# Mixing stage of a hybrid encoder step: the inverse's last level on one quadrant, decay sums of all tiles at once, and three changes of order on GpSimd and VectorE

## What is computed

```
def gdn_chunk(S, q, k, v, g, beta):
    gc = jnp.cumsum(g, axis=-1)
    decay = jnp.exp(jnp.where(lower, gc[..., :, None] - gc[..., None, :], -jnp.inf))
    kb = k * beta[..., None]
    lmat = jnp.where(strict, jnp.einsum('bhid,bhjd->bhij', kb, k) * decay, 0.0)
    t_inv = lax.linalg.triangular_solve(eye + lmat, eye, left_side=True, lower=True, unit_diagonal=True)
    u = t_inv @ (v * beta[..., None])
    w = t_inv @ (kb * jnp.exp(gc)[..., None])
    v_new = u - w @ S
    o = (q * jnp.exp(gc)[..., None]) @ S + (jnp.einsum('bhid,bhjd->bhij', q, k) * decay) @ v_new
    S_new = S * jnp.exp(g_last) + jnp.einsum('bhld,bhle->bhde', k * jnp.exp(g_last - gc), v_new)
```

## Time and profile before

| | us |
|---|---|
| median of 3 runs | 3766.71 (3763.04 to 3767.36) |
| profiled execution, its own time | 3768.46 |
| its span | 3766.8 |
| mixing, iterations without Y ahead of tile 0 | 1427 to 1566 |
| mixing, 23 iterations with all strands | 1604.2 to 2379.3 |
| mixing, 7 iterations without E, F (H in the first only) | 2379.3 to 2589.3 |

### The profile page before, as it was taken

The page is one execution under the profiler, slowest core; times in us unless marked ns, Lnnn a source line. Parts: engine busy times, 40 slices in busy tenths (PEclk is TensorE's granted clock), DMA queues, the critical chain, the costliest instruction groups (busy, mean ns, idle before and its releaser), DMA issues. The chain is left out here.

```text
span 3766.8 us, 66113 instructions
## 1 busy us (share of the span) xinstructions
PE 3191.2 (85%) x18658; PEld 1938.3 (51%) x18659; DVE 2155.4 (57%) x5335; ACT 1538.5 (41%) x3032; POOL 823.0 (22%) x1002
## 2 busy tenths in 40 slices
PE   8997979788797976699999999998499999999920
PEld 3443434333343456577777777766355555555500
DVE  6574757566665764477677777766433333333358
ACT  6464656556555662233333333332122222222222
POOL 0000000000000001255445554553111111111145
PEclk9998989899898985799999999999799999999965
DMA  4456656574747534445554455433367778985378
GB/s 144 142 182 224 213 194 231 184 258 164 274 159 243 190 127 144 121 138 148 145 146 129 130 145 149 131 112 92 132 223 252 269 266 283 324 295 185 110 275 333
DMA packets 487498, 716.00 MB, mean 190 GB/s; under 512 B 92272, under 2 KB 241360, under 8 KB 486992
## 3 DMA queue, kind: packets, MB, share of 16 engines
q1 hardware_dynamic: 404096, 480.63, 41.3%
q10 hardware_dynamic: 54288, 146.56, 9.8%
q0 software_dynamic: 28864, 86.09, 6.3%
HBM read 442.22 MB, written 270.92 MB: 189 GB/s over the span
## 5 line engine op out<-in xcount | busy, mean ns | idle before, releaser
L338 PE MATMUL pP<-h_hi,w_hi 128*128 128x512 f16 (+1 forms) x1728 | 639.0, 374 | 86.1 <-ACT win L430 67.1
L338 PE MATMUL pP<-h_lo,w_hi 128*128 128x512 f16 (+1 forms) x1728 | 637.6, 373 | 0.0
L338 PE MATMUL pP<-h_hi,w_lo 128*128 128x512 f16 (+1 forms) x1728 | 635.9, 372 | 0.0
L1863 PE MATMUL ebank<-w_halves,rowsT_hi 128*128 x1568 | 485.4, 381 | 1.5 <-ACT rowsT_hi L1899 0.9
L529 DVE SCALAR_TENSOR_TENSOR halves<-stage,halves 128x512 f16<-128x512 f32 x384 | 254.6, 687 | 200.6 <-ACT halves L400 200.4
L400 ACT ACTIVATE halves<-stage 128x512 f16<-128x512 f32 x384 | 236.4, 625 | 273.7 <-DMA stage<-in_raw 264.4
L569 DVE SCALAR_TENSOR_TENSOR cv<-win,cols_sb,cv 128x512 f32<-128x512 f32 (+1 forms) x432 | 305.5, 707 | 35.8 <-issue 1.4
L338 PEld LDWEIGHTS pP<-h_hi,w_hi 128*128 128x128 f16 x1728 | 174.6, 101 | 293.1 <-ACT win L430 80.4
L1863 PE MATMUL ebank<-w_halves,rowsT_lo 128*128 x784 | 298.9, 381 | 0.0
L298 POOL TENSOR_TENSOR ss<-ss,eps 128x4 f32<-128x4 f32 (+1 forms) x9 | 2.2, 249 | 1295.7 <-ACT junk L386 1295.7
L338 PEld LDWEIGHTS pP<-h_hi,w_lo 128*128 128x128 f16 x1728 | 175.1, 101 | 191.7 <-issue 18.3
(11 more groups left out here) (344 smaller groups left out, 6666.9 us busy)
## 6 DMA issues: line engine op xcount, KB each, us to landing
stage<-in_raw SPq DMA_DIRECT2D x384, 256.0 KB, 4.0
split<-halves SPq DMA_DIRECT2D x384, 256.0 KB, 3.3
w_halves<-split SPq DMA_DIRECT2D x32, 2048.0 KB, 11.6
y<-yb ACTq DMA_DIRECT2D x98, 512.0 KB, 7.4
ft<-mixin SPq DMA_DIRECT2D x33, 1280.0 KB, 8.5
mixin<-qo ACTq DMA_DIRECT2D x128, 256.0 KB, 3.7
w_halves<-split SPq DMA_DIRECT2D x32, 1024.0 KB, 6.1
xt<-in_x SPq DMA_DIRECT2D x33, 512.0 KB, 5.2
```

What stands on the lines that cost most here:

```text
L338: ins = nc.tensor.matmul(pP[n % NPB][:, 0:N], w[:, k, c0:c0 + P], h[:, k, 0:N], start=(k + i == 0), stop=(k == KD - 1 and i == 2))
L1863: ins = nc.tensor.matmul((M0, M1)[p][:, :], x[p][:, k, :], w[:, bass.ds(s, 1), k, half, :].rearrange("p a n -> p (a n)"), start=(k + i == ...
```

## The change

Three things are done. The decay sums of the 32 prompt tiles are made at the start of mixing, by three matmuls into one bank and three exponentials into `st_all`; `stat`, `gt`, `ex` and `fsc` lose that part for these tiles (the stream tile keeps it). At level 64 the mask, W64, I64, Z64 and its copy work on the one quadrant of 64 by 64 per head that is not known beforehand; Z32's copy now goes to `Zf`, which Z64 reads and completes. And three places of `MIX` change: `eT` comes after `r2`, `B32` before `h2` (both POOL), `on` before `fsc` (DVE).

```diff
-Q.sct0.pool X.eT.pool E.sq.act R.x2.dve Y.KS.pe Y.QS.pe Y.X.dve R.st.act Y.o1.act R.r2.pool X.B16.pool X.eZ.pool
+Q.sct0.pool E.sq.act R.x2.dve Y.KS.pe Y.QS.pe Y.X.dve R.st.act Y.o1.act R.r2.pool X.eT.pool X.B16.pool X.eZ.pool
-E.stat.pe E.sse.dve E.ex.act E.rr.pool Q.sct1.pool R.h2.pool
+E.stat.pe E.sse.dve E.ex.act E.rr.pool Q.sct1.pool X.B32.pool R.h2.pool
-R.lg.pe R.r0.dve X.T16.pe X.T16c.act X.B32.pool R.r1.dve
+R.lg.pe R.r0.dve X.T16.pe X.T16c.act R.r1.dve
-X.W32.pe X.I32.dve F.G.dve E.fsc.dve Y.outA1.pe Y.on.dve
+X.W32.pe X.I32.dve F.G.dve Y.on.dve E.fsc.dve Y.outA1.pe
...
                     for c in range(2 * H):
-                        nc.tensor.matmul(bank[:, c:c + SW], sqb[:, c, :], mat("ones")[:, 0:SW], start=True, stop=True)
-                    pe.wait_ge(*at("gt", t))
-                    c = 2 * H
-                    for m in ("upto_s" if stream else "upto", "after_s" if stream else "after", "ones"):
-                        ins = nc.tensor.matmul(bank[:, c:c + SW], mat(m), gw[:, :], start=True, stop=True)
-                        c += H
+                        ins = nc.tensor.matmul(bank[:, c:c + SW], sqb[:, c, :], mat("ones")[:, 0:SW], start=True, stop=True)
                     if stream:
+                        pe.wait_ge(*at("gt", t))
...
+                        if s == 64:
+                            ins = nc.tensor.matmul(XA[64:P, h, 0:64], Bs[s][0:64, h, 64:P], Tm[0:64, h, 0:64],
+                                                   start=True, stop=True)
...
-                        ins = nc.tensor.matmul(XB[:, h, :], WI[:, h, :], Zm[:, h, :], start=True, stop=True)
+                        ins = nc.tensor.matmul(XB[0:64, h, 64:P], WI[64:P, h, 0:64], Zf[p][64:P, h, 64:P],
+                                               start=True, stop=True)
...
             pe.wait_ge(const_in, 16)
+            for i, m in enumerate(("upto", "after", "ones")):
+                ins = nc.tensor.matmul(flat(XA)[:, i * last * H:(i + 1) * last * H], mat(m), gb[:, 0:last, H:], start=True, stop=True)
+            ins.then_inc(decays_made, 1)
...
                 elif n == "Z64c":
+                    act.wait_ge(*at("Z64", t))
+                    nc.scalar.activation(Zf[p][0:64, :, 64:P], XB[0:64, :, 64:P], ACT.Copy).then_inc(*did(n))
...
+            act.wait_ge(decays_made, 1)
+            for i in range(3):
+                ins = nc.scalar.activation(st_all[:, 0:last, (7 + i) * H:(8 + i) * H],
+                                           flat(XA)[:, i * last * H:(i + 1) * last * H].rearrange("p (t h) -> p t h", h=H), ACT.Exp)
+            ins.then_inc(decays_kept, 1)
...
-                    nc.gpsimd.tensor_tensor(Bs[s][:, :, :], Gin[:, :, :], heads(mat(f"level{s}")), ALU.mult
+                    rows, c0 = (64, 64) if s == 64 else (P, 0)
+                    mask = mat(f"level{s}")[0:rows, c0:P].unsqueeze(1).to_broadcast([rows, H, P - c0])
+                    nc.gpsimd.tensor_tensor(Bs[s][0:rows, :, c0:P], Gin[0:rows, :, c0:P], mask, ALU.mult
...
-                    nc.vector.tensor_copy(gt[p][:, :], gb[:, bass.ds(t, 1), :].rearrange("p a b -> p (a b)"))
-                    dve.drain()
-                    ins = nc.vector.tensor_copy(gw[:, 0:H], gt[p][:, H:])
+                    ins = nc.vector.tensor_copy(gt[p][:, :], gb[:, bass.ds(t, 1), :].rearrange("p a b -> p (a b)"))
...
+                    if n == "I64":
+                        nc.vector.tensor_copy(WI[64:P, :, 0:64], XA[64:P, :, 0:64]).then_inc(*did(n))
```

More of the change, by code:

```diff
@@ L1026, in f_step @@
                     for c in range(2 * H):
-                        nc.tensor.matmul(bank[:, c:c + SW], sqb[:, c, :], mat("ones")[:, 0:SW], start=True, stop=True)
-                    pe.wait_ge(*at("gt", t))
-                    c = 2 * H
-                    for m in ("upto_s" if stream else "upto", "after_s" if stream else "after", "ones"):
-                        ins = nc.tensor.matmul(bank[:, c:c + SW], mat(m), gw[:, :], start=True, stop=True)
-                        c += H
-                    if stream:
+                        ins = nc.tensor.matmul(bank[:, c:c + SW], sqb[:, c, :], mat("ones")[:, 0:SW], start=True, stop=True)
+                    if stream:
+                        pe.wait_ge(*at("gt", t))
+                        c = 2 * H
+                        for m in ("upto_s", "after_s", "ones"):
+                            nc.tensor.matmul(bank[:, c:c + SW], mat(m), gw[:, :], start=True, stop=True)
+                            c += H
                         ins = nc.tensor.matmul(bank[:, c:c + SB * H], mat("ones"),
@@ L1072, in x_step @@
                 elif n == "vt":
+                    pe.wait_ge(decays_kept, 1)
                     pe.wait_ge(*at("I64", t, 1))
@@ L1229, in f_step @@
                     act.wait_ge(*at("sse", t))
-                    ins = nc.scalar.activation(scf[p][:, 7:10, :].rearrange("p a h -> p (a h)"), flat(YE if prologue(t) else FB)[:, 2 * H:5 * H], ACT.Exp)
                     if stream:
-                        ins = nc.scalar.activation(exS[:, :], flat(FB)[:, 5 * H:5 * H + SB * H], ACT.Exp)
-                    ins.then_inc(*did(n))
+                        nc.scalar.activation(scf[p][:, 7:10, :].rearrange("p a h -> p (a h)"), flat(FB)[:, 2 * H:5 * H], ACT.Exp)
+                        nc.scalar.activation(exS[:, :], flat(FB)[:, 5 * H:5 * H + SB * H], ACT.Exp).then_inc(*did(n))
+                    else:
+                        act.sem_inc(*did(n))
                 elif n == "DT":
@@ L1254, in x_step @@
                 elif n == "Z64c":
+                    act.wait_ge(*at("Z64", t))
+                    nc.scalar.activation(Zf[p][0:64, :, 64:P], XB[0:64, :, 64:P], ACT.Copy).then_inc(*did(n))
+                elif n == "Z16c":
+                    act.wait_ge(*at("Z16", t))
+                    nc.scalar.activation(Zm[:, :, :], XA[:, :, :], ACT.Copy).then_inc(*did(n))
+                elif n == "Z32c":
                     act.wait_ge(*at("N", t, 2))
-                    act.wait_ge(*at("Z64", t))
+                    act.wait_ge(*at("Z32", t))
                     nc.scalar.activation(Zf[p][:, :, :], XB[:, :, :], ACT.Copy).then_inc(*did(n))
-                elif n in ("Z16c", "Z32c"):
-                    act.wait_ge(*at(n[:-1], t))
-                    nc.scalar.activation(Zm[:, :, :], (XA if n == "Z16c" else XB)[:, :, :], ACT.Copy).then_inc(*did(n))
                 elif n == "fh":
@@ L1404, in f_step @@
                     dve.wait_ge(*at("stat", t, 1))
-                    nc.vector.tensor_copy(gt[p][:, :], gb[:, bass.ds(t, 1), :].rearrange("p a b -> p (a b)"))
-                    dve.drain()
-                    ins = nc.vector.tensor_copy(gw[:, 0:H], gt[p][:, H:])
+                    ins = nc.vector.tensor_copy(gt[p][:, :], gb[:, bass.ds(t, 1), :].rearrange("p a b -> p (a b)"))
                     if stream:
+                        dve.drain()
+                        nc.vector.tensor_copy(gw[:, 0:H], gt[p][:, H:])
                         ins = nc.vector.tensor_tensor(
@@ L1490, in x_step @@
                     dve.wait_ge(*at(f"W{n[1:]}", t))
-                    nc.vector.tensor_tensor(WI[:, :, :], (XB if n == "I32" else XA)[:, :, :], heads(mat("ident")), ALU.add
-                                            ).then_inc(*did(n))
+                    if n == "I64":
+                        nc.vector.tensor_copy(WI[64:P, :, 0:64], XA[64:P, :, 0:64]).then_inc(*did(n))
+                    else:
+                        nc.vector.tensor_tensor(WI[:, :, :], (XB if n == "I32" else XA)[:, :, :], heads(mat("ident")), ALU.add
+                                                ).then_inc(*did(n))
                 if n == "I64" and stream:
```

18 lines of the change are left out of this document (12 added, 6 removed).

## The result

| | before | after |
|---|---|---|
| median, us (4 runs each) | 3767.03 | 3742.78 (3740.33 to 3743.71) |
| profiled execution, its own time / span | 3768.46 / 3766.8 | 3743.71 / 3742.1 |
| first stat to first KS (ahead of tile 0) | 132.7 | 122.7 |
| iteration of tile 0 | 38.06 | 40.33 |
| 23 iterations with all strands | 775.07 (33.70 each) | 752.45 (32.72 each) |

The ratio is 0.9936 (95% interval 0.9919 to 0.9953): 24 us faster, where 50 were forecast. The stretches are taken between the starts of KS in the two traces, as in the earlier trace rows. The 23 iterations gained 22.6 us instead of 44, 0.98 each instead of 1.9. Ahead of tile 0 it is 10.0 instead of 4; the last seven lost 2.3, where 2 were to be gained, and tile 0's iteration, which the sum leaves out, lost 2.3. (Mixing began 1.8 us later, what follows it took 1.6 longer.)

What follows compares the result with a forecast made beforehand. The prediction took the loop from kt over G to ft's landing, beside PE, as the bound. Gains of 44 (23 iterations), 4 (ahead of tile 0) and 2 (last seven) made 50 us: 3717 us, range 3690 to 3748.

Steps and rivals of the forecast that it cites:

- Ahead of tile 0: Term for the stretch before the first tile: decay sums made at once gain 4 us net, between -2 and +6.
- the last seven: Term for the seven iterations without E and F: 0.3 us gained in each, 2 us together, between -3 and +6.
- the loop: kt to G, then G to ft landed: 33.3 of 33.7 us, falling to 31.8; 1.9 per iteration, 44 us in 23.
- W32's wait: Sign: PE's W32 no longer waits on POOL (1.89 us); T32 waits 1 to 2 us for DVE's I32 instead.
- `on` alone: Step moving `on` before fsc on DVE: oT's wait of 0.73 us goes, but counts nothing by itself.
- xn is short: Sign on DVE: xn takes well below its former duration.
- r2 before eT: Step on POOL: r2 starts at 2009.6, takes 0.95 us; what stood behind both starts 0.4 earlier.
- B32 before h2: Step on POOL: `goh` ends with B32, `esel` meets h2; I32 1.67 us earlier, G 1.5 earlier after kt.
- the signs foretold: Expected in the profile after: `esel` median near 2 us, `goh` below 0.93, `dif` near 0.21, periods 31 to 32.5.
- The first rival: r1 on DVE runs free, `esel` not held by h2; G gains up to 3.5 us: 3680 us, 9%.
- the second rival: The power inside ro on POOL also holds DVE; r1 loses up to 1.0 us more: 3740 us, 12%.
- the fifth rival: Longer pauses of PE ahead of T32 drop its granted clock to the lower level: slower, 3790 us, 5%.

Runs made afterwards that it cites:

- e8_on_only: The kernel before with only `on` moved ahead of fsc on VectorE; ratio 1.0003 to the kernel before.
- e15_drain_h2: The changed kernel with a drain added on GpSimd between B32 and h2; ratio 0.9883 to the kernel before.
- e1_fence: The changed kernel with the drain between r2's two GpSimd instructions replaced by a semaphore; ratio 0.9888 to the kernel before.
- e2_h2late: The changed kernel with h2 behind ro on GpSimd, waiting for r1, and ACT's sh and rx behind T32's copy; ratio 0.9835 to the kernel before.
- The kernel with both POOL edits: The changed kernel with r2's drain replaced by a semaphore and h2 moved behind ro and r1; ratio 0.9789 to the kernel before.
- e14_store_behind: The kernel with both POOL edits, with only G's large store moved behind the load ft on SP; ratio 0.9790 to the kernel before.

## Why the prediction was right and wrong

**Right: the loop, once the change is in.** kt to G (18.9) and G to ft (13.6) make 32.4 of the 32.72 us, kt waits for ft in 12 iterations and KS for `off` in the 11 with V, and what moved G then moved the period: with kt to G of 18.9, 18.2, 18.1, 16.9 and 16.4 the iterations take 32.72, 32.04, 31.84, 31.11 and 30.65. Right too: W32's wait goes and T32 waits for I32 (2.0 us); `on` alone is worth nothing; xn is short (0.85).

In the kernel before the loop was looser than the one iteration that the prediction followed. The means of the 23 are 19.2 and 13.7, 32.9 of 33.70 us, and kt waited for ft once. So of the 0.98 us that an iteration won, G's earlier place gave 0.3 and a quicker landing of ft 0.15; 0.5 is slack in front of kt, of which the sum had counted 0.4. The parts alone on the kernel before keep 0.4 to 0.8 us of that slack, and their period doesn't follow kt to G (e8_on_only: 19.6 and 33.57).

**Wrong, step "r2 before eT".** r2 was to start at ACT's sum and end 0.95 later. It ends 1.0 later than that, since its drain waits for the scatter that it now stands right behind. The step named the queue that r2 leaves (eT) and not the DMA that it comes next to. In the kernel before eT hid that landing, except twice. The term was 0.68 us in 23 iterations, 15.5 us.

**Wrong, step "B32 before h2".** `goh` was to end with B32 and `esel` to meet h2; `goh` stands through both. That costs another 0.88 us in each (e15_drain_h2 against the change), 20 us, and `dif` then meets B64 (0.68 instead of 0.21). G was to come 1.5 us earlier after kt, and 0.3 came; of kt to G, r2's drain takes 0.6 (e1_fence) and h2 right behind B32 takes 0.8 (e15_drain_h2). So `esel` with 0.231, `goh` with 2.999 and `dif` with 0.68 are each against the signs foretold, and the period is just above its 31 to 32.5. The first rival (r1 free) is e2_h2late's state. That the time, 3742.8, lies in the stated range and beside the second rival's 3740 is luck: that rival's cause, the power inside ro, holds nothing up (0.226 beside it), and the loss came from the two steps above.

**Mis-sized.** Ahead of tile 0: 10 instead of 4, 1.1 us in the mean of nine iterations where the sum had 0.5 in seven; how much of it is the matmuls and how much the wait for gw was not taken apart. The last seven: r2's move, which the sum counted at nothing there, costs 9.5. Tile 0's iteration, not in the sum, lost 2.3: PE waits 7.8 us for ft there (7.1 before), and the clock came back later. Over 1570 to 1580, after it had waited, the granted clock was 0.51 (the 1.2 GHz level), over 1578 to 1588 before 0.98; this iteration took 36.1 to 41.9 us in the kernels here.

## What to carry to other kernels

When an instruction is moved in a queue, list what it comes to stand next to, its own drains included: a drain on GpSimd behind a scatter was here a wait for that scatter. A chain of small VectorE instructions loses time where it meets a run of GpSimd multiplications; here it paid to let the long one wait until the chain was done (38 us, e2_h2late). Parts that bring nothing alone can be worth their cycles once another edit takes away the wait that absorbed them, so the edit at the loop goes first. A rival that a row of the kernel before can settle, as the power beside L1593 could, is worth looking up before it gets a chance. The kernel with both POOL edits, 2.1% faster than before, is the best here, level with e14_store_behind.

## What the runs showed of the hardware

A GpSimd drain held until an indirect DMA that the engine had issued had landed, up to 3.4 us in one case, and went on 0.17 us later; a semaphore between the same two instructions didn't.

On VectorE `goh`, which came up to 0.69 us before the end of a GpSimd mask, stood through the multiplication behind it as well when that followed without a pause (94 of 94); a drain that left a pause of 0.25 us let it in. `dif` and `esel`, which came 0.73 to 1.29 us before the border of two masks, were let in there without a pause (114 of 114). Beside a GpSimd power of 128x4, 1.04 us long, a VectorE instruction with two inputs in SBUF took its free 0.226 us.

In the kernel with `off` ahead of V, PE's granted clock fell to 0.94 in the mean. A stretch of it, and weight loads of one iteration:

```profile
1700.00:1900.00 200.00, 187.27 (x1317) 150.08 (x1316) 134.45 (x538) 73.34 (x201) 103.39 (x129) 0.94 0.47 141
```

```profile
1890.57 1.78 PEld L1151 LDWEIGHTS bank<-xb,Zf 128*128 128x128 f32 x8 [2.96 <-issue]
1892.23 3.53 PEld L1034 LDWEIGHTS bank<-const,kz 128*128 128x128 f32 x16
1895.64 1.83 PEld L1167 LDWEIGHTS bank<-vdec,ktok 128*128 128x128 f32 x8
```

Behind a pause of 2.96 us the 16 passes take 3.53 us and eight 1.83, twice the 1.87 and 0.97 at a clock of 1.00: the 1.2 instead of the 2.4 GHz level. That is the fifth rival, which the change itself, whose pauses of PE in the 23 iterations stay at 2.1 us, didn't meet there.
